# Gate products of a mixing stage as seven half-size block products, with the projections ahead of them and kept on chip

## What is computed

```python
y_hy = hyena_branch(hy_cols, p) @ p['hy_proj']            # (512 tokens, 512) @ (512, 1024)
y_rw, finals = rwkv_branch(rw_cols, p, states0)
g_hy, g_rw = jnp.split(jax.nn.sigmoid(gate_cols), 2, axis=-1)   # gate_cols = h @ w_in[:, gates], h is (512, 1024)
mixed = (g_hy * y_hy + g_rw * (y_rw @ p['rw_proj'])) @ p['w_out']
```

## Time and profile before

| | us |
|---|---|
| median of 3 runs | 3606.65 |
| profiled execution, whole | 3609.94 |
| profiled execution, span | 3608.2 |
| TensorE busy in the span | 3281.7 (91%) |
| VectorE busy | 1456.1 (40%) |
| ScalarE busy | 619.8 (17%) |
| gate products of the stage, busy | 112.9 |

### The profile page before, as it was taken

How to read it: one execution, slowest core, us unless ns; L and a number is a source line. 1 busy time by engine, 2 the same in 40 slices (tenths; PEclk the granted TensorE clock), 3 DMA queues, 4 the chain that set the end, 5 groups by cost and what they waited for, 6 DMA issues and landing times. The chain is left out here.

```text
span 3608.2 us, 49891 instructions
## 1 busy us (share of the span) xinstructions
PE 3281.7 (91%) x21661; PEld 1750.7 (49%) x21661; DVE 1456.1 (40%) x2603; ACT 619.8 (17%) x1226; POOL 8.0 (0%) x40
## 2 busy tenths in 40 slices
PE   6978899898997988899989899989999976999998
PEld 3557787544444333333333343455444434468853
DVE  2255666444113000000000135752666674157776
ACT  2133332110012000000000122161222003031200
POOL 0000000000000000000000000000000000000000
PEclk9989999899997999999999999999999997999999
DMA  6134444311225999999999921102333564212233
GB/s 245 48 122 146 164 146 148 132 58 35 88 82 240 430 430 430 431 430 427 426 430 426 380 74 47 49 22 63 135 120 129 171 186 187 70 66 75 94 134 128
DMA packets 202974, 689.83 MB, mean 191 GB/s; under 512 B 31240, under 2 KB 96252, under 8 KB 176517
## 3 DMA queue, kind: packets, MB, share of 16 engines
q1 hardware_dynamic: 201768, 686.28, 48.8%
q10 hardware_dynamic: 989, 0.36, 0.0%
HBM read 661.94 MB, written 22.31 MB: 190 GB/s over the span
## 5 line engine op out<-in xcount | busy, mean ns | idle before, releaser
L2073 PE MATMUL banks<-weight_ring,xe_T 128*64 128x512 f32 x1312 | 295.3, 596 | 42.1 <-DMA weight_ring<-in_exp_w 39.9
L2846 PE MATMUL banks<-h_T,weight_ring 128*128 128x512 f32 x704 | 306.5, 594 | 2.1 <-PEq L91 2.1
L2846 PEld LDWEIGHTS banks<-h_T,weight_ring 128*128 128x128 f32 x704 | 132.2, 190 | 163.1 <-issue 163.0
L2073 PEld LDWEIGHTS banks<-weight_ring,xe_T 128*64 128x64 f32 x1312 | 90.3, 137 | 234.4 <-issue 159.4
L2089 PE MATMUL banks<-weight_ring,hid_T 128*64 128x512 f32 x656 | 147.0, 596 | 12.0 <-DMA weight_ring<-in_exp_w 12.0
L2409 PE MATMUL banks<-h_T,weight_ring 128*128 128x512 f32 x320 | 142.1, 597 | 0.0
L2073 PE MATMUL banks<-h_T,xe_T 128*64 128x512 f32 x464 | 105.5, 596 | 17.7 <-DMA h_T<-in_exp_w 17.6
L1722 PE MATMUL banks<-h_T,weight_ring 128*128 128x512 f32 x256 | 112.9, 600 | 3.9 <-PEq L91 3.9
L3774 PE MATMUL banks<-weight_ring,h_T 128*128 128x512 f32 x256 | 113.0, 603 | 2.6 <-PEq L91 2.6
L3139 DVE SCALAR_TENSOR_TENSOR conv<-banks,cols,conv 128x511 f32<-128x511 f32 (+1 forms) x96 | 71.9, 749 | 100.4 <-ACT conv L2986 97.8
L2236 DVE TENSOR_TENSOR hid<-silu,banks 128x1024 f32<-128x1024 f32 x16 | 19.5, 1221 | 222.9 <-issue 179.9
(11 more groups left out here) (665 smaller groups left out, 5231.6 us busy)
## 6 DMA issues: line engine op xcount, KB each, us to landing
weight_ring<-in_exp_w SPq DMA_DIRECT2D x123, 2048.0 KB, 15.7
h_T<-in_exp_w SPq DMA_DIRECT2D x41, 2048.0 KB, 15.7
weight_ring<-in_ada_w SPq DMA_DIRECT2D x24, 2048.0 KB, 8.8
weight_ring<-in_ffn_w_up SPq DMA_DIRECT2D x44, 1024.0 KB, 6.3
weight_ring<-in_ffn_w_down SPq DMA_DIRECT2D x20, 2048.0 KB, 7.7
expert_out<-in_exp_w SPq DMA_DIRECT2D x19, 2048.0 KB, 19.1
weight_ring<-in_mod_w SPq DMA_DIRECT2D x12, 2048.0 KB, 8.6
spare<-in_exp_w SPq DMA_DIRECT2D x9, 2048.0 KB, 20.5
```

What stands on the lines that cost most here:

```text
L2073: mm = pe.matmul(k.ps[64 * half:64 * half + 64, 2 * c + b % 2, :], R.rows[:, e // 2 % 2, kt, (e % 2) * CAP:(e % 2 + 1) * CAP], w[:, r, 512 ...
L2846: mm = pe.matmul(k.ps[:, b + c, :], w[:, c, kt, m * P:m * P + P], hT[:, kt, :], start=kt == 0, stop=kt == 7)
```

## The change

`mix_branches` alone changes; the list of chunks and the ring stay as they are.
- A unit is now one branch c of one pair j: 256 gate channels by 512 tokens. Its product of 1024 contraction channels is split in 2x2 blocks on each side and made as seven products of blocks (4 contraction tiles, 128 channels, 256 tokens each), in the order 1, 6, 7, 5, 2, 4, 3, from sums of weight blocks (`wsum`) and of token blocks (`hsum`).
- The four projections of a pair come ahead of its first unit, are evicted by ScalarE, and wait in SBUF (`shares`).
- Banks are taken in turn, eight groups round; a group waits for whoever read the group eight places before it.
- ScalarE evicts product 1, VectorE joins the seven into the four blocks of `gates` in SBUF; ScalarE takes the sigmoid there in place (1024 elements), VectorE multiplies by the projections and adds the two branches.
- Both chunks of a pair are released by ScalarE, in one `sem_inc` of 2 behind the sigmoid of the pair's second unit.

More of the change, by code:

```diff
@@ L1711, in _ @@
         def _(pe):
-            for i in range(DT):
-                j, m, b = i // 2, i % 2, 4 * (i % 2)
-                if m == 0:
-                    k.ring.wait(pe, 2 * j)
[L1716 to L1731, removed]
+            def bank_free(e):
+                if e not in behind:
+                    return
+                last = behind[e]
[3 more added lines that the diff above has]
+                    pe.wait_ge(taken, last[1] + 1)
+                else:
+                    pe.wait_ge(joined, JOINS * last[1] + {6: 1, 7: 2, 5: 4, 2: 5, 4: 6, 3: 7}[last[2]])
@@ new lines, in project @@
+            def project(j):
+                k.ring.wait(pe, 2 * j + 1)
+                wp = k.ring.chunk(2 * j + 1)[:, 0:2048].rearrange("p (c k n) -> p c k n", c=2, k=4)
+                for n in range(4):
+                    c, t = n // 2, n % 2
+                    bank_free(("projected", 4 * j + n))
+                    for kt in range(4):
+                        mm = pe.matmul(k.ps[:, bank["projected", 4 * j + n], :], wp[:, c, kt, t * P:t * P + P], (hy, rw)[c][:, kt, :],
+                                       start=kt == 0, stop=kt == 3)
+                    mm.then_inc(projected, 1)
@@ new lines, in block_sum @@
+            def block_sum(u, n, left, right):
+                bank_free(("part", u, n))
+                for kt in range(4):
+                    mm = pe.matmul(ps(u, n), left[:, kt, :], right[:, kt, :], start=kt == 0, stop=kt == 3)
+                mm.then_inc(parts, 1)
+            for u in range(len(units)):
+                j, c = units[u]
+                if c == 0:
+                    project(j)
+                    k.ring.wait(pe, 2 * j)
+                a11, a12, a21, a22 = unit_blocks(u)
+                b11, b12, b21, b22 = token_blocks()
+                block_sum(u, 1, a11, b11)
+                pe.wait_ge(readied, 2 * u + 2)
+                block_sum(u, 6, wsum[:, 1], hsum[:, 1])
+                block_sum(u, 7, wsum[:, 2], hsum[:, 2])
+                block_sum(u, 5, wsum[:, 0], hsum[:, 0])
+                block_sum(u, 2, a12, b21)
+                block_sum(u, 4, a22, hsum[:, 3])
+                pe.wait_ge(readied, 2 * u + 3)
+                block_sum(u, 3, wsum[:, 3], b22)
@@ L1733, in _ @@
         @block.scalar
         def _(act):
[L1735 to L1742, removed]
+            def sigmoid(u):
+                j, c = units[u]
+                act.wait_ge(joined, JOINS * u + JOINS)
+                act.activation(gates[:, c, :, :], gates[:, c, :, :], ACT.Sigmoid).then_inc(sigmoids, 1)
+                if c:
+                    act.sem_inc(k.ring.used, 2)
@@ L1746, in _, with token_sums @@
             link = Chain(dve, linked)
[L1747 to L1751, removed]
+            def token_sums():
+                b11, b12, b21, b22 = token_blocks()
+                link(dve.tensor_tensor(hsum[:, 0], b12, b11, ALU.subtract))
+                link(dve.tensor_tensor(hsum[:, 1], b22, hsum[:, 0], ALU.subtract))
+                link(dve.tensor_tensor(hsum[:, 2], b22, b12, ALU.subtract))
+                dve.tensor_tensor(hsum[:, 3], hsum[:, 1], b21, ALU.subtract).then_inc(readied, 1)
@@ new lines, in gated @@
+            def gated(u):
+                j, c = units[u]
+                dve.wait_ge(sigmoids, u + 1)
+                dve.wait_ge(kept, 4 * j + 4)
+                for t in range(2):
+                    link(dve.tensor_tensor(gates[:, c, t, :], gates[:, c, t, :], shares[:, c, t, :], ALU.mult))
+                    if c:
+                        dve.tensor_tensor(mixed[:, 2 * j + t, :], gates[:, 0, t, :], gates[:, 1, t, :], ALU.add).then_inc(mixed_done, 1)
+            token_sums()
+            unit_sums(0)
@@ new lines, in _, with put @@
+            last_unit_sum(0)
+            for u in range(len(units)):
+                j, c = units[u]
+                def put(out, left, right, op=ALU.add):
+                    dve.tensor_tensor(out, left, right, op).then_inc(joined, 1)
+                if u:
+                    last_unit_sum(u)
+                    if c == 0:
+                        gated(u - 1)
+                dve.wait_ge(taken, u + 1)
+                dve.wait_ge(parts, 7 * u + 2)
+                put(u2, m1, ps(u, 6))
+                dve.wait_ge(parts, 7 * u + 3)
+                dve.wait_ge(joined, JOINS * u + 1)
+                put(u3, u2, ps(u, 7))
+                if c:
+                    gated(u - 1)
+                dve.wait_ge(parts, 7 * u + 4)
+                dve.wait_ge(joined, JOINS * u + 2)
+                put(gates[:, c, 1, high], u3, ps(u, 5))
+                put(u2, u2, ps(u, 5))
+                if u + 1 < len(units):
+                    unit_sums(u + 1)
+                dve.wait_ge(parts, 7 * u + 5)
+                put(gates[:, c, 0, low], m1, ps(u, 2))
+                dve.wait_ge(parts, 7 * u + 6)
+                put(gates[:, c, 1, low], u3, ps(u, 4), ALU.subtract)
+                dve.wait_ge(parts, 7 * u + 7)
+                dve.wait_ge(joined, JOINS * u + 4)
+                put(gates[:, c, 0, high], u2, ps(u, 3))
```

27 lines of the change are left out of this document (25 added, 2 removed).

## The result

The changed kernel takes 3616.84 us (median of 9 runs, 3613.03 to 3620.84) against 3607.42 us for the kernel before in the same series (9 runs, 3604.43 to 3612.32). The ratio is 1.0024, 95% interval 1.0016 to 1.0032: slower by 8.7 us (5.8 to 11.5); the two medians lie 9.4 us apart. The forecast was 11.1 us slower, 3617.7. A later series of the same two kernels gave 1.0034 (1.0021 to 1.0046).

What follows compares the result with a forecast made beforehand. TensorE, busy for 91% of the span, was taken as the bound. Terms: -13.1 + 1.4 + 3 x (5.8 + 1.8) = +11.1 us, taking the median from 3606.65 to 3617.7 us, range 3611 to 3626.

Steps and rivals of the forecast that it cites:

- Block products, -13.1: TensorE in the changed stage: seven block products replace plain gate products, saving 3.29 us a pair, 13.1 us a stage.
- VectorE and banks at nothing: Inside the pairs: joins, sums and bank reuse lie beside TensorE's work and were costed at nothing.
- The wait, 5.8 us: Between pairs, three times: TensorE waits for the next projection chunk, 5.8 us each, bounds 5.45 to 7.2.
- The clock, 1.8 us: Behind each of three waits: TensorE's clock falls to half, losing 1.8 us; from below nothing, from above double.
- The sign given: Sign of being right: each TensorE gap ahead of projections followed by about 4 us at a clock near 0.6.
- The end, +1.4: Stage's end: join, sigmoid and four dependent operations take 4.7 us against 3.3 before, plus 1.4 us.
- The faster one: Rival at the first product of pairs 2 to 4: projection chunk not late, -11.7 us, 3594.9; chance 0.06.
- The clock did not hold: Rival behind the waits: the wait comes but the clock holds, +5.7 us, 3612.4, no measurable change; chance 0.06.
- Transfers did not share in full: Rival: transfers share the engines, each wait grows by about 4 us, time to 3630; 0.07 together with table reloads.
- one table load: Rival: ScalarE reloads its table between Copy and Sigmoid, +3.8 to +5 us, 3622; 0.07 together with shared transfers.
- Weight loads do not stick out: Rival on TensorE in this stage: 192 more weight loads of 0.190 us exposed, 36 us, 3654; chance 0.01.
- Nothing else moved: Sign of being right: the stage is longer by 11 us and nothing else in the kernel moves.

Runs made afterwards that it cites:

- e1: Changed kernel with each pair's projection chunk loaded before its gate chunk, each released after its last reader; stage 158.68 us, 0.9976 of the kernel before.
- e4: Kernel before, plain gate products, but projections first in each tile and both chunks released together by ScalarE; stage 192.53 us, ratio 1.0059.
- e2: Changed kernel with both chunks of a pair released earlier, behind block 4 of its second unit; stage 171.01 us, 1.0012 of the kernel before.
- e5: Kernel before in its own order, with only the gate chunk released late by ScalarE together with the projection chunk; stage 170.66 us, ratio 0.9995.
- e6: e1 plus the last unit's sigmoid in two halves, finished half first; stage 157.48 us, 0.9950 of the kernel before.
- e3: Changed kernel with six unused matmuls added ahead of the projection wait of pairs 2 to 4; stage 176.37 us, 1.0024 of the kernel before.
- e8: Repeat of e3, measured beside the changed kernel; stage 175.79 us, 1.0018 of the kernel before.

## Why the prediction was right

- **Block products, -13.1.** Measured -13.15 as the remainder, -13.12 directly. The rate read from the last layer's unit holds to the hundredth: 1.73 us a block. Weight loads of 0.190 us hide here as they do there. The rule of the Trainium skill that the prediction weighed against that (TensorE: Matmul & The Clock Gate, Part 3, "The mechanism") isn't borne out in this stage either; the same section also lets a load into the background weight buffer run ahead, which the prediction left out.
- **VectorE and banks at nothing.** Right; no gap inside a pair, and in e1 none in the whole stage.
- **The wait, 5.8 us.** Measured 5.54 to 5.87. Its steps (join at 0.2, release at 0.7, second half 0.4 later, landing 4.3 and some slip) came out one by one; the slip from the gate transfers behind was 0.4, against 0.3 taken. Reading the release as going out at dispatch was worth 1 us a gap.
- **The clock, 1.8 us.** Measured 1.73, 2.86 and 1.90, a sum of 6.5 against 5.4. The largest miss of the sum. The two gaps before happened to cost the same; over all traces the cost varies from 1.5 to 3.2 us, and the gap's length does not order it (in e4 gaps of 4.90, 4.95 and 5.07 us cost 1.7, 1.6 and 3.2). The sign given, about 4 us at a clock near 0.6, fits the first gap; behind the second it was 5.9 us at 0.52.
- **The end, +1.4.** Measured +1.24.
- **Rivals.** The faster one needed the chunk in time: all three gaps end by in_rw_proj. The clock did not hold. Transfers did not share in full, since rw_proj landed after 4.7 us while the gates took 9.5. There is one table load in the stage, as before (1.3 us). Weight loads do not stick out.
- **The whole.** 8.7 and 12.3 us in two series, 11.6 and 11.6 in the stage. "Nothing else moved" did not come true. The profiled executions' spans differ by 6.6 us only: ahead of the stage the changed kernel is 0.7 us shorter, and behind it 4.3 us (2572.2 us from the first `w_out` product to the end, against 2576.5 before). That the median came within 1 us of 3617.7 is therefore partly luck. Over the ten traces the part ahead of the stage, whose engine programs are the same in all, takes from 856.05 to 864.79 us, and the part behind it from 2572.0 to 2577.8. One piece of the 4.3 can be named: 1.7 us of it is a half-clock phase that the kernel before has behind an idle gap of 2.08 us and the changed kernel, behind a gap of the same length, has not (before, then changed):

```profile
2062.10 2.56 PE L1840 MATMUL banks<-expert_out,slots_T 128*128 128x512 f32 x4 [2.08 <-PEq L91]
2064.46 3.01 PE L1846 MATMUL banks<-spare,square 128*128 128x512 f32 x4
...
2071.15 1.96 PE L1965 MATMUL banks<-expert_out,slots_T 128*128 128x512 f32 x4 [2.08 <-PEq L91]
2072.94 1.88 PE L1971 MATMUL banks<-spare,square 128*128 128x512 f32 x4
```

The rest of it stays open.

## What to carry to other kernels

When a step is moved ahead of another, look in the load queue for the chunk that it reads and ask who frees that chunk's place: in this ring of three places, with two chunks a step, a step that read first the chunk loaded last had to wait. A margin in a ring belongs to order and release together, so a change of either has to be checked against the time from first issue to last landing (here 5.1 us) even where the DMAs are busy for a quarter of the stage. And a wait of TensorE of 5 to 6 us cost 6.7 to 8.7 in these traces, because the work behind it started at half clock.

## What the runs showed of the hardware

- The granted clock stays at full well into an idle gap (0.99 over 5.4 us, 0.89 over 5.7, 0.72 over 5.5), and the slow phase lies mostly behind it.
- The length of a gap does not by itself tell whether the clock falls. Every idle gap of 3.9 us or more at the edges of this stage and inside it was followed by slow records, in all ten traces; e2's gaps of 3.2, 3.2 and 3.3 us once in three. But behind the gap of 2.08 us ahead of the product of the experts' outputs (at 2062.10 in the kernel before, lines above) there were slow records in four traces (before, e2, e5 and e6) and none in the other six.
- The slow phase isn't constant: behind the gaps of this stage it cost 1.5 to 3.2 us (10.04 us at most for sixteen records where 7.03 is full speed, 6.77 for eight where 3.60 is).
- A wait for DMA is as long with TensorE busy as idle: 5.5 to 6.2 us in the six filled ones of e3 and e8, 5.5 to 5.9 in the three without. Six matmuls without use at each of three boundaries shortened the stage by 5.9 and 6.5 us.
